# Attention of a two-layer encoder: output halves added one step earlier, and the work of a head put in another order

## The reference, cut to what matters

```python
def mla_mixer(u, w_in, q_norm, kv_norm, w_q_up, w_kv_up, q_head_norm, k_head_norm, w_out):
    c_q, c_kv, k_rope = jnp.split(u @ w_in, [Q_LORA_RANK, Q_LORA_RANK + KV_LORA_RANK], axis=-1)
    q = (rmsnorm(c_q, q_norm) @ w_q_up).reshape(b, L, MLA_HEADS, QK_HEAD_DIM)
    kv = (rmsnorm(c_kv, kv_norm) @ w_kv_up).reshape(b, L, MLA_HEADS, QK_NOPE_DIM + V_HEAD_DIM)
    ...
    q = apply_rope(rmsnorm(q, q_head_norm), pos)
    k = apply_rope(rmsnorm(k, k_head_norm), pos)
    o = block_attention(q, k, v)
    return o.reshape(b, L, MLA_HEADS * V_HEAD_DIM) @ w_out
```

## Time and profile before

| | |
|---|---|
| Median of 3 runs | 3036.17 us (3033.82 to 3037.96) |
| Profiled execution | 3037.44 us, span 3035.7 us |
| PE busy | 2925.2 us, 96% |
| PEld busy | 2636.4 us, 87% |
| DVE busy | 1882.6 us, 62% |
| ACT busy | 1186.8 us, 39% |
| POOL busy | 1764.9 us, 58% |
| Chain that ended last | PE 74%, POOL 7%, DVE 7%, issue 5%, ACT 4%, DMA 2% |

### The profile page before, as it was taken

How to read it: one execution, slowest core, us unless ns; L and a number is a source line. 1 busy time by engine, 2 the same in 40 slices (tenths; PEclk the granted TensorE clock), 3 DMA queues, 4 the chain that set the end, 5 groups by cost and what they waited for, 6 DMA issues and landing times.

```text
span 3035.7 us, 47763 instructions
## 1 busy us (share of the span) xinstructions
PE 2925.2 (96%) x18181; PEld 2636.4 (87%) x18181; DVE 1882.6 (62%) x2920; ACT 1186.8 (39%) x2060; POOL 1764.9 (58%) x1122
## 2 busy tenths in 40 slices
PE   8999989899999999999999999999999999999998
PEld 8988888889999999999999978677777788888776
DVE  6566666655543446777788851677778844445666
ACT  4466666632333334553111122222323533334552
POOL 4434554453777677675344443467674577776774
PEclk9989999999999999999999999999999999999998
DMA  3011110121222334442333423332323233325432
GB/s 128 26 37 34 44 34 23 37 99 42 89 92 93 99 101 166 153 130 66 101 116 93 132 84 118 120 123 94 124 94 122 66 105 104 102 98 179 145 128 90
DMA packets 200167, 290.44 MB, mean 96 GB/s; under 512 B 17159, under 2 KB 109319, under 8 KB 199943
## 3 DMA queue, kind: packets, MB, share of 16 engines
q1 hardware_dynamic: 160338, 240.07, 24.4%
q10 hardware_dynamic: 39605, 47.34, 4.6%
HBM read 212.43 MB, written 74.92 MB: 95 GB/s over the span
## 4 chain that ended last, share of the span: by engine, by line
PE 74%; POOL 7%; DVE 7%; issue 5%; ACT 4%; DMA 2%; SPq 1%; POOLq 0%; ACTq 0%; DVEq 0%
PE PS L1419 71%; DMA Wraw<-in_w 2%; PE PS L1670 2%; POOL Wlo L1255 1%; ACT PTH L2478 1%; POOL Wlo L1315 1%; ACT PR L2488 1%; PE PS L2036 1%; SPq L975 1%; POOL SQ L1360 1%; DVE PR L3172 0%; DVE GD L3797 0%; POOL RMS L1325 0%; POOL Wraw L1273 0%; POOL Wraw L1271 0%
## 5 line engine op out<-in xcount | busy, mean ns | idle before, releaser
L1419 PE MATMUL PS<-Uhi,Whi 128*128 128x352 f32 (+2 forms) x2028 | 513.5, 329 | 16.8 <-DVE Ulo L2953 13.8
L1419 PE MATMUL PS<-Uhi,Wlo 128*128 128x352 f32 (+2 forms) x2028 | 508.4, 326 | 0.0
L1419 PE MATMUL PS<-Ulo,Whi 128*128 128x352 f32 (+2 forms) x2028 | 507.3, 326 | 0.0
L1255 POOL TENSOR_TENSOR Wlo<-Wraw,Whi 128x512 fp32r<-128x512 f32 x242 | 329.8, 1367 | 133.9 <-ACT Whi L2596 130.0
L1133 POOL TENSOR_TENSOR Whi<-Wraw,const 128x1024 fp32r<-128x1024 f32 x64 | 158.4, 2474 | 423.8 <-PE PS L1419 408.9
L1419 PEld LDWEIGHTS PS<-Uhi,Whi 128*128 128x128 f32 x2028 | 341.9, 190 | 39.5 <-issue 15.7
L1419 PEld LDWEIGHTS PS<-Uhi,Wlo 128*128 128x128 f32 x2028 | 344.5, 189 | 19.5
L1419 PEld LDWEIGHTS PS<-Ulo,Whi 128*128 128x128 f32 x2028 | 343.7, 189 | 20.0
L2596 ACT ACTIVATE Whi<-Wraw 128x512 fp32r<-128x512 f32 x242 | 151.2, 628 | 329.5 <-POOL Wraw L1273 136.1
L1419 PE MATMUL PS<-T,Whi 128*128 128x264 f32 (+1 forms) x1328 | 218.8, 288 | 2.1 <-DVE H L3481 1.9
L1419 PEld LDWEIGHTS PS<-T,Whi 128*128 128x128 f32 x1328 | 186.3, 188 | 2.9 <-DVE H L3481 2.3
(11 more groups left out here) (447 smaller groups left out, 7337.3 us busy)
## 6 DMA issues: line engine op xcount, KB each, us to landing
Wraw<-in_w SPq DMA_DIRECT2D x192, 256.0 KB, 2.9
Wraw<-in_w SPq DMA_DIRECT2D x91, 512.0 KB, 3.9
Wraw<-in_w SPq DMA_DIRECT2D x168, 128.0 KB, 2.7
xt<-XTT ACTq DMA_DIRECT2D x20, 640.0 KB, 5.6
opd<-HID SPq DMA_DIRECT2D x40, 264.0 KB, 3.4
T<-opd SPq DMA_DIRECT2D x18, 528.0 KB, 4.1
Ulo<-opd SPq DMA_DIRECT2D x17, 528.0 KB, 4.7
Ulo<-opd SPq DMA_DIRECT2D x17, 512.0 KB, 5.7
```

The source lines that it names most:

```text
L1255: pool.tensor_tensor(f.oplo[j % SLOTS], FIRST_S2 if (p, k) == (0, 6) else f.factors[k], f.ophi[j % SLOTS].bitcast(F32), ALU.subtract).then ...
L1419: ins = pe.matmul(out, lhsT, rhs, start=start, stop=stop, skip_group_check=True)
```

## The change

ScalarE's `take_k` and `take_q` are split in copy and square. The copy of an output half moves to the start of the next step, and its sum behind `low_turned` of the next step, where it came one step later, ahead of the maximum. TensorE's query projections go to steps 0 to 3, query norms to steps 4 and 5, key projections from steps 5 and 7 to 7 and 8, key norms from 8 and 9 to 9 and step 0 of the next head. ScalarE takes queries at steps 2 and 4 and keys at 8 and 9; high values, high queries and high weights move to later steps. VectorE's `query_factors` has three parts, at steps 6, 7 and 8. On GpSimd, `scale_outputs` moves ahead of `turn_queries`, and the low weights of odd heads behind `low_k`. `high_k` for all heads but head 0 was on GpSimd and stays there.

```diff
--- before.py
+++ after.py
@@ -1236,17 +1236,20 @@
                 low_k(nxt)
             if nxt % 4:
                 low_values(nxt)
+            if j >= 4 and j % 2 == 0:
+                scale_outputs(j // 2 - 2)
             turn_queries(nxt)
+            if nxt % 2:
+                if split_unit(j) is not None:
+                    low_weights(j)
+                low_q(nxt)
+                continue
+            scale_keys(nxt)
+            low_q(nxt)
+            high_k(nxt)
+            low_k(nxt)
             if split_unit(j) is not None:
                 low_weights(j)
-            if nxt % 2 == 0:
-                scale_keys(nxt)
-            low_q(nxt)
-            if nxt % 2 == 0:
-                high_k(nxt)
-                low_k(nxt)
-            if j >= 4 and j % 2 == 0:
-                scale_outputs(j // 2 - 2)
 
         def low_factor(f, j):
 
@@ -1738,21 +1741,19 @@
                         turn_factors(nxt // 2)
                     if nxt % 2 and j and n == 2:
                         turn_sums(j // 2 - 1)
-                    if n == 0:
-                        project_q(nxt, 0, 0)
-                        project_q(nxt, 0, 1)
-                    if n in (1, 2):
-                        project_q(nxt, 1, n - 1)
-                    if n == 3:
-                        query_norms(nxt, 0)
-                        query_norms(nxt, 1)
+                    if n == 0 and nxt % 2 == 0:
+                        key_norms(nxt // 2, 1)
+                    if n < 4:
+                        project_q(nxt, n // 2, n % 2)
+                    elif n < 6:
+                        query_norms(nxt, n - 4)
                     if nxt % 4 == 0 and n >= 5:
                         project_v(nxt // 4, n - 5)
                     if nxt % 2 and nxt + 1 < HEADS:
-                        if n in (5, 7):
-                            project_k((nxt + 1) // 2, n // 7)
-                        if n >= 8:
-                            key_norms((nxt + 1) // 2, n - 8)
+                        if n in (7, 8):
+                            project_k((nxt + 1) // 2, n - 7)
+                        if n == 9:
+                            key_norms((nxt + 1) // 2, 0)
         t = HEADS * PER_HEAD
         turn_probs(t - 1)
         pe.wait_ge(stats_taken, len(STATS))
@@ -2410,13 +2411,17 @@
 
             return ap[:, s * L:(s + 1) * L].rearrange("p (h n) -> p h n", h=2)
 
-        def take_k(p, s, bank=A_PREP):
+        def square_k(p, s, bank=A_PREP):
 
             halves = pair(bank)
             act.wait_ge(prep_full, PREP["k", p, s] + 1)
             if p:
                 act.wait_ge(stats_full, STATS["q", 2 * p - 1] + 1)
             act.activation(of_seq(SQ[:], s), halves, ACT.Square).then_inc(k_squared, 1)
+
+        def copy_k(p, s, bank=A_PREP):
+
+            halves = pair(bank)
             if p:
                 act.wait_ge(k_scaled, 2 * (2 * p - 1))
             act.activation(of_seq(KR[0][0:NOPE, :], s), halves[0:NOPE], ACT.Copy, scale=col("k_nope")[0:NOPE])\
@@ -2428,6 +2433,9 @@
             if x >= 2:
                 act.wait_ge(sc_full, (x - 1) * PER_HEAD)
             act.activation(of_seq(QS[x % 2], s), pair(bank), ACT.Copy).then_inc(prep_taken, 1)
+
+        def square_q(x, s):
+
             act.wait_ge(prep_taken, PREP["q", x, s] + 1)
             act.wait_ge(stats_full, STATS["q", x - 1] + 1 if x % 2 else STATS["k", x // 2] + 1)
             act.activation(SQ[:, s * L:(s + 1) * L], QS[x % 2][:, s * L:(s + 1) * L], ACT.Square).then_inc(q_squared, 1)
@@ -2503,12 +2511,14 @@
             act.activation(Ohi[:, k, :], H[:, k, :], ACT.Copy).then_inc(hi_ready, c.adds(hi_ready))
 
         for s in range(NSEQ):
-            take_k(0, s, 2 * s)
+            square_k(0, s, 2 * s)
+            copy_k(0, s, 2 * s)
         act.wait_ge(pair_full, 1)
         act.activation(banks(KR[0][NOPE:P, :]), PS[NOPE:P, 4:7, 0:NT], ACT.Copy).then_inc(act_steps, c.adds(act_steps))
         act.activation(banks(KR[1][0:P - NOPE, :]), PS[0:P - NOPE, 4:7, 0:NT], ACT.Copy).then_inc(pair_taken, 1)
         for s in range(NSEQ):
             take_q(0, s, 2 * s)
+            square_q(0, s)
         high_q(0)
         high_k(0)
         high_values(0)
@@ -2516,26 +2526,32 @@
             nxt = j + 1
             for n in range(PER_HEAD):
                 t = j * PER_HEAD + n
-                if nxt < HEADS:
-                    if n in (1, 3):
-                        take_q(nxt, n // 3)
-                    if nxt % 2 and nxt + 1 < HEADS and n in (6, 8):
-                        take_k((nxt + 1) // 2, n // 8)
+                more_k = nxt % 2 and nxt + 1 < HEADS
+                if half_at_turn(t, 1):
+                    other_half(*half_at_turn(t, 1))
+                if nxt < HEADS and n in (2, 4):
+                    take_q(nxt, n // 2 - 1)
+                if more_k and n in (8, 9):
+                    square_k((nxt + 1) // 2, n - 8)
+                if more_k and n == 8:
+                    copy_k((nxt + 1) // 2, 0)
                 if t >= 1:
                     high_turned(t - 1)
                 exponentials_of(t)
-                if half_at_turn(t, 1):
-                    other_half(*half_at_turn(t, 1))
                 if j and j % 4 == 0 and n == 1:
                     high_values(j)
                 if nxt < HEADS:
-                    if n == 2 and nxt % 4:
+                    if n in (2, 4):
+                        square_q(nxt, n // 2 - 1)
+                    if n == 3 and nxt % 4:
                         high_values(nxt)
-                    if n == 5:
+                    if n == 6:
                         high_q(nxt)
+                    if more_k and n == 9:
+                        copy_k((nxt + 1) // 2, 1)
                 elif n < PAIRS - 1:
                     high_out(n)
-                if j >= 0 and split_unit(j) is not None and n == 4:
+                if split_unit(j) is not None and n == (7 if j % 2 else 5):
                     high_weights(j)
         t = HEADS * PER_HEAD
         high_turned(t - 1)
@@ -3119,9 +3135,9 @@
                 if x >= 2:
                     vec.wait_ge(p_full, (x - 1) * PER_HEAD)
                 chain_seed(y, v, a, -1)
+            if part < 2:
                 chain_round(y, v, a)
                 return
-            chain_round(y, v, a)
             chain_product(y, v, a)
             vec.scalar_tensor_tensor(y, a, 1.5, y, ALU.add, ALU.mult).then_inc(qs_ready, 1)
 
@@ -3226,6 +3242,7 @@
         take_v(0, 1, 3)
         take_v(0, 2, 2)
         query_factors(0, 1)
+        query_factors(0, 2)
         take_v(0, 3)
         take_v(0, 4, 6)
         for j in range(HEADS):
@@ -3240,20 +3257,22 @@
                     take_factors(nxt // 2)
                 if nxt < HEADS and nxt % 2 and j and n == 3:
                     take_sums(j // 2 - 1)
-                if nxt % 2 and nxt + 1 < HEADS and n in (6, 8):
-                    take_k((nxt + 1) // 2, n // 8)
-                if half_at_turn(t, 2):
-                    add_outputs(*half_at_turn(t, 2))
+                if nxt % 2 and nxt + 1 < HEADS and n == 8:
+                    take_k((nxt + 1) // 2, 0)
                 maximum(t)
                 if t >= 1:
                     low_turned(t - 1)
+                if half_at_turn(t, 1):
+                    add_outputs(*half_at_turn(t, 1))
+                if nxt % 2 and nxt + 1 < HEADS and n == 9:
+                    take_k((nxt + 1) // 2, 1)
                 if j and j % 2 == 0 and n == 1:
                     invert(j // 2 - 1)
                 if nxt < HEADS:
                     if nxt % 2 == 0 and n < 2:
                         key_factors(nxt // 2, n)
-                    if n in (4, 5):
-                        query_factors(nxt, n == 5)
+                    if n in (6, 7, 8):
+                        query_factors(nxt, n - 6)
         t = HEADS * PER_HEAD
         invert(PAIRS - 1)
         low_turned(t - 1)
```

## The result

The changed kernel takes 2982.49 us (median of 4, 2979.8 to 2986.22), beside 3034.99 for the kernel before on the same chip: ratio 0.9828, 95% interval 0.9811 to 0.9845. That is 52 us less (47 to 57). Forecast were 39 less, 2997, in a range from 2978 to 3021. The two profiled executions lie further apart than the medians, 3035.7 and 2978.0 us of span: 57.7 in place of 52.

The account below looks back on a forecast made before the run. TensorE, busy 96% of the span, bounds the kernel, so only its waits in attention can pay. Savings 16.4 + 20.1 + 4 + 8.8 - 8 = 41, taken as 39, make the median of 3036.17 us 2997; range 2978 to 3021.

Parts of the forecast that it names:

- rival 3: Attention: no low clock at all and no tail stall in plain heads, another 20 us gained, 2977; chance 0.06.
- Work per head: TensorE's own work at 2.4 GHz in attention: 109.0 us in four heads taking 129.76, so 20.8 us is loss.
- Halves at no cost: Output halves: ScalarE's earlier copy is made while scores run and costs nothing; the 14.7 us wait for the sum goes.
- Projections and norms spread: Steps 0 to 3 hold 10.3 us with nothing to wait for; the 5.8 us wait for the squares goes.
- Key projections at 7 and 8: Second projection waits 1.1 us for copies of the first, plus 0.3 for ScalarE's bunching: 1.4 per key head.
- Low weights: Heads 0, 4, 8, 12: GpSimd's low part is ready at 20.4 where 19.5 is wanted; 1.0 us of wait stays.
- Plain heads: Heads without key or value projections, like 5: 23.9 plus 2.9 stall in steps 4 to 9 plus 0.6 low-key wait, 27.4 us.
- Value heads: Heads that project values, like 7: VectorE takes the values late by 0.5 us at step 8; 31.7 us in all.
- The clock: Attention: one low 4 us stretch per four heads in place of two or three, at 2 us; 8 us charged.
- 1: Steps 5 to 9: ScalarE's queue makes transposes late, 1.3 us more per head, 20 less saved, 3017; chance 0.16.
- 2: Attention: all stalls move and none goes, so no change, 3036; chance 0.04.
- 4: Steps 7 to 9 of every head: small idles keep the clock at 0.84, slower at 3059; chance 0.06.

Follow-up runs that it names:

- order alone: The changed kernel with the output halves put back as before, keeping the new order of the head; 2988.48 us, ratio 0.9847 to the kernel before.
- the two shifted ones: The kernel before with 20 or 40 matmuls that nobody reads, once, ahead of the first head; 3040.29 us and 3037.31 us.
- filled: The kernel before with five unread matmuls added at the end of TensorE's steps 5, 7 and 8 of heads 1, 5, 9 and 13; 3041.21 us, ratio 1.0019.

## Why the prediction was right, and where its sum was off

**That only TensorE's waits can pay, all in attention.** Right: 53.7 of the 57.7 us between the spans lie there.

The number came out at the edge, though. The saving of 52 us is the upper end of the class that the forecast gave 0.68 (25 to 52); the range, which took in rival 3 down to 2978, held it with 4 us to spare. The sum of its savings was 41, and attention in the profiles saved 53.7.

**Work per head.** Right to 3 us: the prediction had 109.0 us of work in four heads, and the loss against it went from 20.8 to 7.4. The windows have TensorE busy for 111.7 at a clock of 1.00, so 2.7 of these 7.4 are work and 4.7 idle, where 12.3 were idle before. (A step is a block of 106 queries, not of keys, as the prediction calls it. Its 60 matmuls of a value head are 7.6 by its own 0.127, not 7.4.)

**Halves at no cost.** Right. VectorE's wait for the copy fell from 17.4 us to 2.0, once, in the last head. That the sum stood behind `query_factors` is one reason for its wait: the order alone brings TensorE's wait for the sum to 2.4 us, and the spread queries alone to 5.7. The prediction gave each wait to one edit. The runs show that several belong to either: the squares' wait goes with the halves alone.

**Projections and norms spread.** Right: steps 0 to 3 take 10.5 us in head 4 and 10.6 in head 6, for 10.3. Alone this part, with the key projections where they were, is worth 10 us.

**Key projections at 7 and 8.** The wait is there in each of seven key heads, but 0.47 to 0.59 us and not 1.1: VectorE's copy ends some 1.7 us behind the first projection, not 2.3. The bunching of ScalarE, for which 0.3 was added, did not come; in head 8 it stood idle ahead of the square, and VectorE waited for nothing but that square:

```profile
373.30 0.61 ACT L2420 ACTIVATE SQ<-PS 128x528 f32<-128x528 f32 x1 [0.76 <-PE PS L1422]
```

```profile
374.00 0.78 DVE L3076 TENSOR_SCALAR KR<-PS,cols 64x528 f32<-64x528 f32 x1 [0.78 <-ACT SQ L2420]
```

**Low weights.** 0.70 where 1.0 was forecast (0.9 by its own 20.4 - 19.5), and 0.17 in head 0; the part of `scale_outputs` in it is 0.53.

**Plain heads.** 3.1 us over the 23.9 of work (forecast 2.9), of which 1.73 are waits in the trace and the rest work that 23.9 left out; 0.77 of wait for the low keys (forecast 0.6); 27.77 in all (forecast 27.4). What the moved low weights would cost if they stood in front was not worked out there; it is 27 us.

**Value heads.** 31.90 for 31.7, with 0.36 of wait for the values at step 8, as named.

**The clock: mis-sized.** The sum charged 8 us for low stretches after the change, two for each plain head. Measured are 3.4 in all of attention, 1.7 of them behind a plain head. Of four plain heads only head 1 ends at a low clock; that "the plain heads' tails stay at 1.2 GHz" does not hold in heads 5, 9 and 13, with their waits of 0.64 and 1.09. What the clock cost before was counted as gain only as far as heads 5 to 8, the pattern, carry it. Heads 0 and 1 lost more: head 0 went from 34.2 to 26.8 us, 7.4 for the 4.1 of its kind, head 1 from 31.2 to 28.2. Head by head, the 12.4 us between the sum (41.3) and the profiles (53.7) are 7.8 in the four plain heads, 3.3 in head 0 and 2.9 in the other six key heads, less 1.5 in the value heads, head 14 and head 15. The 2 us taken off "for what a walk misses" weren't needed. So the term that was mis-sized is the clock; the waits were sized to within 0.6 us a head.

**Rivals.** 1, 2 and 4 are out by time. Rival 3 had the sign of the miss, but only half of its mechanism: the tails' stalls stayed, the clock's didn't. The rule on frequent small idles, from the Trainium skill's page "TensorE: Matmul & The Clock Gate" ("A second HAM failure mode: psum-queue depth-cycling"), agrees with the kernel before (0.62 at 312) and not with the changed one, whose heads 5 to 8 have waits of 0.36 to 1.09 us and a clock of 1.00.

**What stays open.** Which idle times make the clock fall. Over a third of the gain is the clock's, and the runs show its cause only in the large. By the single profiles the kernels with 42 to 55 us of idle time in attention lost 15 to 43 us (before, the two shifted ones, queries alone, filled), and those with 20 to 27 lost 0 to 12 (the changed kernel and its variants, halves alone, order alone); only the one with the low weights first, with its waits of over 6 us, is in neither group. Within these groups idle time does not order them: 42 idle went with 25.6 lost in one kernel and 42.7 in another, 27 with 11.9 and with 1.7. Each program has one profile, which can't tell a program's share from an execution's.

## What to carry to other kernels

Where several engines meet in a program of fixed order, write down what each step holds and walk it through with measured durations: the lengths of heads 5 to 8 came out within 0.6 us each. But don't give each wait to one edit: two edits that were worth 34 and 46 us alone gave 52 together, and one (the queries) was worth 10 without its partner. And when operations of a half-idle engine change places, ask which of them ends the chain that the next stage starts with: one low part ahead of the keys cost 27 us, waits and clock together.

## What the runs showed of the hardware

TensorE's granted clock in a stretch with waits of 0.5 to 2.3 us is not a property of the program alone. Nineteen runs of the kernel before on one chip have mean clocks from 0.982 to 0.988 and times from 3029 to 3042 us; ten runs of the filled kernel have 0.979 to 0.987 and 3031 to 3051 us. Four runs of the changed kernel, with about half the idle time in attention, have 0.989 to 0.992 and 2980 to 2986 us. So a single profile of a kernel with many such waits can mislead by some 10 us in 3000 about what an edit is worth, and a thin step in it about which step to mend. The clock of every run says more than the windows of one.
